# Two-block network on one core: the experts' combining and the norm behind it as one stage

## The reference, cut to what matters

```python
for l in range(DEPTH_2):
    ...
    y = hier_moe(tokens, w_rg[l], b_rg[l], w_re[l], b_re[l], w1[l], w3[l], w2[l])
    if not last:
        ctx = layer_norm(ALPHA * ctx + mod_c[5] * y[b_ * s_:].reshape(b_, c_len, d_), ln2_g[l], ln2_b[l])
    x = layer_norm(ALPHA * x + g2 * y[:b_ * s_].reshape(b_, s_, d_), ln2_g[l], ln2_b[l])
```

## Time and profile before

| | us |
|---|---|
| median of 3 runs | 3180.1 (3175.82 to 3185.31) |
| the profiled execution, its own time | 3182.42 |
| span of the profiled execution | 3180.4 |
| layer 0: first gather to the mixer's first matmul | 2265.84 to 2341.86 |
| layer 1: first gather to the end of the span | 3123.82 to 3180.4 |
| mean granted TensorE clock over the execution | 0.933 |

### The profile page before, as it was taken

One profiled execution on the slowest core, in us unless ns is written; L12 is line 12 of the kernel. 1 busy time (PEld: TensorE's weight loads), 2 busy tenths in 40 slices (PEclk: granted clock), 3 DMA queues, 4 the chain that ended last, 5 costly groups with the idle time before them and its releaser, 6 DMA issues. The chain is left out here.

```text
span 3180.4 us, 42124 instructions
## 1 busy us (share of the span) xinstructions
PE 2760.8 (87%) x16138; PEld 1567.9 (49%) x16139; DVE 1065.4 (33%) x2245; ACT 678.0 (21%) x1400; POOL 149.3 (5%) x209
## 2 busy tenths in 40 slices
PE   6999998898999998998984999989689884798765
PEld 3444556564444475556653555445354642354433
DVE  2330156526877303026244111111332624222114
ACT  2440148510000010116331000000131712010002
POOL 0000000000000000000001100000100000121101
PEclk9999989999999999998996999999789896899987
DMA  4223120118655422101014889999632013999994
GB/s 174 99 80 97 51 93 21 43 73 243 248 223 206 176 89 77 56 27 60 27 47 186 341 358 409 410 412 390 240 123 80 34 59 146 363 365 383 401 418 146
DMA packets 137306, 594.43 MB, mean 187 GB/s; under 512 B 20336, under 2 KB 40588, under 8 KB 90608
## 3 DMA queue, kind: packets, MB, share of 16 engines
q1 hardware_dynamic: 86704, 359.25, 30.2%
q10 hardware_dynamic: 41808, 212.75, 16.8%
q0 software_dynamic: 8688, 21.00, 1.9%
HBM read 574.06 MB, written 33.69 MB: 191 GB/s over the span
## 5 line engine op out<-in xcount | busy, mean ns | idle before, releaser
L159 PE MATMUL psum<-normed,weight_ring 128*128 128x512 f32 (+1 forms) x1536 | 644.5, 581 | 26.5 <-DMA weight_ring<-in_w_ffn_dram 14.3
L159 PEld LDWEIGHTS psum<-normed,weight_ring 128*128 128x128 f32 x1536 | 294.8, 192 | 371.3 <-issue 352.9
L1110 DVE SCALAR_TENSOR_TENSOR psum<-weight_ring,condition_rows 128x1024 f32<-128x1024 f32 x192 | 236.9, 1234 | 15.0 <-issue 0.4
L159 PE MATMUL psum<-modulated,weight_ring 128*128 128x384 f32 (+2 forms) x640 | 228.7, 518 | 0.0
L2326 PE MATMUL psum<-weight_ring,slot_rows_turned 128*64 128x256 f32 x1792 | 205.9, 383 | 0.6 <-issue 0.6
L2337 PE MATMUL psum<-weight_ring,slot_rows_turned 128*32 128x256 f32 x2176 | 143.7, 409 | 68.2 <-DMA weight_ring<-in_w_dram 46.8
L2488 DVE COPY expert_hidden_turned<-psum 128x128 f32<-128x128 f32 (+1 forms) x93 | 32.7, 352 | 466.8 <-PE psum L2348 466.8
L159 PEld LDWEIGHTS psum<-modulated,weight_ring 128*128 128x128 f32 x640 | 121.4, 190 | 105.5 <-issue 51.0
L2355 PE MATMUL psum<-weight_ring,expert_hidden_turned 128*32 128x256 f32 (+1 forms) x1536 | 168.0, 445 | 0.0
L2326 PEld LDWEIGHTS psum<-weight_ring,slot_rows_turned 128*64 128x64 f32 x1792 | 127.7, 138 | 76.3 <-issue 17.2
L2418 ACT ACTIVATE expert_silu<-psum 64x256 f32<-64x256 f32 (+1 forms) x91 | 34.6, 381 | 602.8 <-PE psum L2326 320.7
(11 more groups left out here) (396 smaller groups left out, 3193.8 us busy)
## 6 DMA issues: line engine op xcount, KB each, us to landing
third_stream_weights<-in_w_dram ACTq DMA_DIRECT2D x93, 2048.0 KB, 14.9
weight_ring<-in_w_dram SPq DMA_DIRECT2D x84, 2048.0 KB, 11.5
weight_ring<-in_w_ada_dram SPq DMA_DIRECT2D x24, 2048.0 KB, 11.4
weight_ring<-in_w_ffn_dram SPq DMA_DIRECT2D x11, 2048.0 KB, 7.6
weight_ring<-in_w_rnn_dram SPq DMA_DIRECT2D x8, 1536.0 KB, 11.6
weight_ring<-in_w_att_dram SPq DMA_DIRECT2D x6, 2048.0 KB, 7.7
weight_ring<-in_w_in_dram SPq DMA_DIRECT2D x6, 2048.0 KB, 10.4
weight_ring<-in_w_down_dram SPq DMA_DIRECT2D x8, 1408.0 KB, 6.3
```

Of the source, the lines that this page charges most:

```text
L159: last = nc.tensor.matmul(out, weights[:, k * P:(k + 1) * P], rhs(k), start=(k == 0), stop=(k == tiles - 1))
L1110: last = nc.vector.scalar_tensor_tensor(out=product, in0=w[:, t], scalar=1.0, in1=CR[:, v, :], op0=ALU.mult, op1=ALU.mult, accum_out=c.mod ...
```

## The change

`combine` and the `layer_norm` behind it become one function and one block, `combine_and_norm`. It has NBUF = 4 buffer pairs in both layers: in layer 0 they are cut out of the mixer's empty tiles `MIX` and `VG`, in layer 1 they are a tensor of eight rows. Transposed tiles have two places in PSUM (`turned_at`) instead of four, so that the means and variances have banks of their own. TensorE takes mean 0 right behind the transpose of tile 3, and each further mean as soon as `added` says that its two tiles are in the residual. VectorE centres piece 0 ahead of adds 4 and 5. SyncE's feed lies in the same block as the norm. The routing tables `R` live on until the mixer of the next layer is done, and two transfer semaphores are shared. The other norms keep `layer_norm`.

```diff
-def combine(c, l, R, nt, parts):
+def combine_and_norm(c, l, R, nt, rows, gain, bias, modulated=None, store=None):
...
     nc, ps, X = c.nc, c.ps, c.X
-    NBUF = 3
+    NBUF = len(rows) // 2
+    Y1, Y2 = rows[:NBUF], rows[NBUF:]
+    WIDTH = 256
+    npiece = nt * P // WIDTH
+    rows_in = [c.sig(f"combine_rows_landed{b}") for b in range(NBUF)]
+    weighted, combined = c.sig("combine_weighted"), c.sig("combine_done")
+    turned, added = c.sig("combine_turned"), c.sig("combine_added")
...
+        VAR = sb("ln_var", [P, 2, nt * P])
+        if modulated:
+            HX, to, which = modulated
+            SQ = HX
...
+        turned_at = lambda i, k: ps[:, 4 + 2 * (i % 2) + k // 4, (k % 4) * P:(k % 4 + 1) * P]
         with nc.Block() as block:
...
                 for i in range(nt):
                     if i >= NBUF:
                         turned.wait(pool, i - NBUF + 1)
-                    for k, dst in enumerate((Y1, Y2)):
-                        pool.indirect_dma_start(dst[:, i % NBUF, :], None, c.expert_out,
+                    for k, y in enumerate((Y1[i % NBUF], Y2[i % NBUF])):
+                        pool.indirect_dma_start(y, None, c.expert_out,
                                                 bass.IndirectOffsetOnAxis(R.slot[:, k, i:i + 1], 0))\
                             .then_inc(rows_in[i % NBUF].sem, 16)
...
+            @block.tensor
+            def _(pe):
+                def turn(i):
+                    combined.wait(pe, i + 1)
+                    if i >= 2:
+                        added.wait(pe, i - 1)
+                    for k in range(KT):
+                        last = nc.tensor.transpose(turned_at(i, k), Y1[i % NBUF][:, k * P:(k + 1) * P], c.ident[:, :])
+                    last.then_inc(turned.sem, 1)
+
+                def mean(i):
+                    added.wait(pe, 2 * i + 2)
+                    for k in range(KT):
+                        last = nc.tensor.matmul(ps[:, i, 0:WIDTH], c.mean_w[:, :], X[:, k, cols(i)],
+                                                start=(k == 0), stop=(k == KT - 1))
+                    last.then_inc(mean_ready.sem, 1)
+
+                def variance(i):
+                    squared.wait(pe, i + 1)
+                    for k in range(KT):
+                        last = nc.tensor.matmul(ps[:, i, 0:WIDTH], c.mean_w[:, :], SQ[:, k, cols(i)],
+                                                start=(k == 0), stop=(k == KT - 1))
+                    last.then_inc(var_ready.sem, 1)
+
                 for i in range(nt):
-                    rows_in[i % NBUF].wait(act, 32 * (i // NBUF + 1))
-                    y = Y1[:, i % NBUF, :]
-                    nc.scalar.activation(y, y, ACT.Copy, scale=R.gate[:, 0, i:i + 1]).then_inc(weighted.sem, 1)
+                    turn(i)
+                    if i == 3:
+                        mean(0)
+                for i in range(1, npiece):
+                    mean(i)
+                    variance(i - 1)
+                variance(npiece - 1)
 
...
-                for step in range(nt + 1):
-                    if step < nt:
-                        weighted.wait(dve, step + 1)
-                        y = Y1[:, step % NBUF, :]
-                        v.scalar_tensor_tensor(out=y, in0=Y2[:, step % NBUF, :], scalar=R.gate[:, 1, step:step + 1],
-                                               in1=y, op0=ALU.mult, op1=ALU.add).then_inc(combined.sem, 1)
-                    if step >= 1:
+
+                def combine(i):
+                    weighted.wait(dve, i + 1)
+                    y = Y1[i % NBUF]
+                    v.scalar_tensor_tensor(out=y, in0=Y2[i % NBUF], scalar=R.gate[:, 1, i:i + 1], in1=y,
+                                           op0=ALU.mult, op1=ALU.add).then_inc(combined.sem, 1)
+
+                def add(i):
+                    vv = 0 if i < ST else 1
+                    turned.wait(dve, i + 1)
+                    for k in range(KT):
+                        x = X[:, k, i * P:(i + 1) * P]
+                        last = v.scalar_tensor_tensor(out=x, in0=turned_at(i, k), scalar=c.mod[:, l, 40 + k, vv:vv + 1],
+                                                      in1=x, op0=ALU.mult, op1=ALU.add)
+                    last.then_inc(added.sem, 1)
+
+                def centre(i):
+                    mean_ready.wait(dve, i + 1)
+                    x = X[:, :, cols(i)]
+                    v.tensor_tensor(x, x, ps[:, i, 0:WIDTH].unsqueeze(1).broadcast_to([P, KT, WIDTH]),
+                                    ALU.subtract).then_inc(centred.sem, 1)
...
+                def scale(i):
+                    rooted.wait(dve, i + 1)
+                    v.reciprocal(VAR[:, 1, cols(i)], VAR[:, 0, cols(i)])
...
+                def modulate(i):
+                    shifted.wait(dve, i + 1)
...
+                combine(0)
+                for i in range(1, 4):
+                    combine(i)
+                    add(i - 1)
+                if nt > 4:
+                    combine(4)
+                add(3)
+                if nt > 4:
+                    combine(5)
+                centre(0)
+                for i in range(4, nt):
+                    add(i)
+                for step in range(1, npiece + 3):
+                    if step < npiece:
+                        centre(step)
+                    if 2 <= step < npiece + 2:
+                        scale(step - 2)
+                    if modulated and step >= 3:
+                        modulate(step - 3)
+
+            @block.scalar
...
+                for i in range(nt):
+                    rows_in[i % NBUF].wait(act, 32 * (i // NBUF + 1))
+                    y = Y1[i % NBUF]
+                    a.activation(y, y, ACT.Copy, scale=R.gate[:, 0, i:i + 1]).then_inc(weighted.sem, 1)
+                for step in range(npiece + 2):
+                    if step < npiece:
+                        centred.wait(act, step + 1)
+                        a.activation(SQ[:, :, cols(step)], X[:, :, cols(step)], ACT.Square).then_inc(squared.sem, 1)
+                    if 1 <= step < npiece + 1:
...
+                    if step >= 2:
+                        i = step - 2
                         for k in range(KT):
...
-            @block.tensor
-            def _(pe):
-                for i in range(nt):
-                    combined.wait(pe, i + 1)
-                    if i >= 4:
-                        added.wait(pe, i - 3)
-                    for k in range(KT):
-                        last = nc.tensor.transpose(ps[:, 2 * (i % 4) + k // 4, (k % 4) * P:(k % 4 + 1) * P],
-                                                   Y1[:, i % NBUF, k * P:(k + 1) * P], c.ident[:, :])
-                    last.then_inc(turned.sem, 1)
...
             @block.sync
             def _(sp):
                 combined.wait(sp, nt)
                 c.ring.feed(sp, c.ring.uses + Ring.SLOTS)
-        for q in range(NBUF):
-            rows_in[q].passed(32 * len(range(q, nt, NBUF)))
-        for s in (weighted, combined, turned, added):
-            s.passed(nt)
+                if store:
+                    for i in range(npiece):
...
+                    store.wait(sp, 16 * npiece)
...
+        routing.close()
         nt = sum(n for _, n in parts) // P
-        with ExitStack() as ctx:
-            R = Routing(c, ctx, l)
-            with ExitStack() as moe:
-                HX = sb("moe_in", [P, KT, T], l, moe)
-                router = Router(c, moe, l)
-                layer_norm(c, nt * P, f"ln1_g{l}", f"ln1_b{l}", (HX, l, 3), router)
-                route(c, l, router, R, nt)
-            experts(c, l, R, nt)
-            combine(c, l, R, nt, parts)
+        routing = ExitStack()
+        R = Routing(c, routing, l)
+        with ExitStack() as moe:
+            HX = sb("moe_in", [P, KT, T], l, moe)
+            router = Router(c, moe, l)
+            layer_norm(c, nt * P, f"ln1_g{l}", f"ln1_b{l}", (HX, l, 3), router)
+            route(c, l, router, R, nt)
+        experts(c, l, R, nt)
         if l < NL - 1:
             outer, inner, (MIX, K, VG), HX = mixer_buffers(l + 1)
-            layer_norm(c, nt * P, f"ln2_g{l}", f"ln2_b{l}", (HX, l + 1, 0))
+            free = [x.rearrange("p a b -> p (a b)") for x in (MIX[:, :, :], VG[:, :, :])]
+            rows = [x[:, r * D:(r + 1) * D] for x in free for r in range(x.shape[1] // D)]
+            combine_and_norm(c, l, R, nt, rows, f"ln2_g{l}", f"ln2_b{l}", (HX, l + 1, 0))
         else:
-            layer_norm(c, nt * P, f"ln2_g{l}", f"ln2_b{l}", store=c.sem("out_stored"))
+            Y = sb("choice_rows", [P, 2 * nt, D], l, routing)
+            combine_and_norm(c, l, R, nt, [Y[:, r, :] for r in range(2 * nt)], f"ln2_g{l}", f"ln2_b{l}",
+                             store=c.sig("stage_transfers_landed"))
+            routing.close()
```

More of the change, by code:

```diff
@@ L2581, in _ @@
                 v = nc.vector
-                for step in range(nt + 1):
-                    if step < nt:
-                        weighted.wait(dve, step + 1)
```

(43 more changed lines are left out.)

35 lines of the change are left out of this document (27 added, 8 removed).

## The result

The changed kernel takes 3159.5 us (median of 4 runs, 3158.87 to 3160.37), the kernel before 3179.9 us (median of 4, 3175.82 to 3185.31): a ratio of 0.9932 with a 95% interval from 0.9918 to 0.9947, so it is faster by 0.7%. The forecast was 3160; it had counted 22.3 us of gain, and the two medians are 20.5 us apart. The profiled execution took 3160.37 us, its span 3158.5.

What follows compares the result with a forecast made beforehand. TensorE (busy 87%) and the weights it waits for bound the program, but the change touches two stretches where TensorE is mostly idle. Gains of 16.4 us (layer 0) and 5.9 (layer 1), 22.3 off 3182.4, give 3160 us, range 3151 to 3172.

Steps and rivals of the forecast that it cites:

- The bound of the stage: Layer 0: time is set by when the third centring starts, 16.4 us earlier, plus an unchanged 21.6 us.
- stage 0: Layer 0, first gather to the mixer's first matmul: forecast 59.6 us instead of 76.0.
- tail of 21.6 us: Layer 0, third centring's start to the mixer's first matmul: same instructions in the same order, so all the gain arrives.
- The gathers: Both layers: seventh unheld, eighth held by a combine; layer 0's last tile lands at 2288.6 instead of 2291.1.
- The rival with both gathers held: Both layers: combines hold the seventh and eighth gathers, costing 1.7 us per layer, 3163.6 us in all; chance 0.07.
- The seam: Layer 0, last add to first mean: SyncE's weight loads hold the next block until 2302.30; worth nothing in layer 1.
- Mean 0 and the clock: Both layers, first mean behind tile 3's transpose: clock rises after 3.6 us, leaving 1.6 us low; mean costs 4.4 us.
- Everything arrives downstream: Behind layer 0's norm: mixer weights are there by 2324, so the gain is kept; rival that it is lost, 0.03.
- stage 1: Layer 1, first gather to the end of the span: forecast 50.7 us, against 56.6 before.

Runs made afterwards that it cites:

- run with the root ahead: Changed kernel with layer 0's norm reordered: root 0 before squares 1 on ScalarE, scaling 0 before centring 2 on VectorE; 3160.2 us, ratio 0.9939.
- run with the loads moved: Kernel before, with SyncE's six weight loads moved from the combining block to the norm's block behind it; 3177.0 us, ratio 0.9991.
- run with both: Kernel before with four buffer pairs and the weight loads in the norm's block, still two blocks in the old order; 3169.2 us, ratio 0.9969.
- run with the norm behind: Changed kernel, but in layer 0 mean 0 behind all transposes and centring 0 behind all adds; 3164.0 us, ratio 0.9956.

## Why the prediction was right

**The bound of the stage.** That stage 0 is the way to centring 2 plus a tail of 21.6 us held to a tenth in the change (38.0 and 21.6). The run with the root ahead shows the limit of it: the tail is not fixed (20.0 us there), it hangs on variance 2, and I had called it VectorE's alone.

**The gathers.** The eighth ran into combine 0 and ended 0.81 us behind it (2274.18), as priced; the seventh was not held. Tile 5 was weighted at 22.0 us of the stage, against 22.8 forecast. The rival with both gathers held is out.

**The seam.** Right in place and size: 4.6 us forecast, and the gap shrank by 4.6 in the run with the loads moved and by 4.5 in the run with both. The stages gained 4.2 each time, alone with a last add 0.8 us sooner and a mean 0 that was 1.1 slower. In layer 1 it was worth nothing, as said.

**Mean 0 and the clock.** Here a term was mis-sized. I counted 3.6 us from transpose 3's start; the clock took 4.9, and mean 0 cost 5.2 instead of 4.4 (5.0 until transpose 4), with 3.1 us at the low level where I had 1.6. In layer 0 this was made up around it: transpose 3 held TensorE for 1.76 us until the mean, not 1.97, transposes 4 and 5 took 1.75 until mean 1 instead of 2.0, and three pieces followed each other every 3.45 instead of 3.5; with them centring 2 came at 38.0, as forecast. In layer 1 it was made up by rows that came sooner: combine 0 was at 7.4 us of the stage instead of 8.0, and mean 0 0.6 us earlier than I had it. The forecast of 22.3 us is met by the measured 22.3 of both stages through errors that cancel, each under 1 us. The mechanism was right; that the sum agrees to a tenth is luck, and so is a median within 1 us of 3160, since the stretches that no edit touches scatter by more.

**Everything arrives downstream.** The mixer started on its weights at once, and the stretch between the stages is 2.0 us longer, within its scatter over all runs of 5.7 us.

**Where the gain was.** My sum went from start to end and had no shares. The experiments give them for stage 0, in the order in which they were put on: four pairs 3.0, loads out of the seam 4.2, one block with a mean that waits for its own two tiles 4.8, norm ahead of the last two tiles 4.4; together 16.4. For stage 1, pairs 2.3 and the one block 3.7; but the old code of stage 1 took 54.9 us in the run with the loads moved, and against that the pairs bring 0.6. Taken off again at the end, the pairs are worth only 1.1 and 1.0 by the stages, so the shares depend on the order. Each share is a difference of two single executions, and the rise of the clock alone moves one by up to 1.6 us.

**What stays open.** Why the clock rises after 2.7 to 5.9 us of work in different runs. How much of that belongs to an edit is not shown: the two profiles of the changed kernel have 4.9 and 4.7 us in layer 0, 4.7 and 4.2 in layer 1. Mean 0 cost 4.1 us right behind transpose 5 in one block, and up to 6.7 at the start of a block, for the same 8 matmuls. Open too is whether three pairs cost the whole kernel the 2 us of the stages or the 8 us of the ratios.

## What to carry to other kernels

A boundary between two blocks costs what the last queue in it still has to do; look for a sequencer that only issues transfers there, and give it a block with cover. Where a reduction over pieces follows a loop over tiles, let it start on the first piece's tiles and not behind the loop: here that and the one block brought 9 of 16 us, and more buffers, which look like the obvious cure for the waiting gathers, brought 3 alone and 1 at the end by the stage's time. Before moving work into an idle gap, ask what that work is ahead of on its engine, and what an engine that now waits longer does to its clock: filling 3.5 us of VectorE's idle time made variance 2 late and slow and gave nothing.

## What the runs showed of the hardware

The clock of TensorE did not rise a fixed time after the work began. With no gap over 0.3 us in it, it rose 3.7 and 3.6 us after the start in the two norms of the kernel before, 4.9 and 4.7 after transpose 3 began in the change, 3.3 and 3.8 with three pairs, 5.3 and 4.8 with the early root, 5.9 and 3.2 after the mean began in the run with the loads moved, and 2.7 us after transpose 5 in the run with the norm behind. A forecast should carry some 1.5 us up and down for it. Where mean 0 stands right behind transpose 3 and no work was added (nine stages of five profiles), the rise came 23.4 to 24.2 us behind the first gather, although transpose 3 began anywhere from 18.6 to 20.9; so in these kernels the place in the stage was the better guide than the start of the unbroken work. It is not general either: with mean 0 behind transpose 5 the rise came at 27.8.

A gather that runs beside a combine is held only if it begins well inside it. Over the twelve profiles, the 44 gathers that began 0.27 to 1.19 us after a combine's start all ended 0.80 to 0.85 us behind its end, those at 2273.05 and 2275.67 in the change among them (1.13 and 1.83 us). Those that began before a combine took the usual 0.93 or 0.94 and the combine 1.27 to 1.29, and so nearly did the two that began at most 0.08 us after it: 0.94 at 3115.39 in the change, with a combine of 1.33, and 0.93 with one of 1.30 in the run with the loads moved. The rule of the Trainium skill ("SBUF — State Buffer", section "SBUF: two separate sides": the later one fully blocks) agrees with the 44 in that the gather waits for the combine, though it also ends 0.8 us behind; the combines that began inside a gather, and were not held, contradict it.
